# Early modulation in quarter chunks with three of four summed on VectorE, and the SSD projection in four batches, in a two-block hybrid mixer and expert kernel

## The reference, cut to what matters

```python
mod = silu(c) @ ada_w + ada_b            # ada_w is 1024 x 6144: six parts of 1024
shift, scale = mod[0:1024], mod[1024:2048]   # the other four parts are used later
h = rms_norm(x, norm1_g) * (1 + scale) + shift
z = h @ w_in                             # w_in is 1024 wide in, cut in columns by use
xbc = silu(causal_conv4(z[:, 5136:6672]) + bias)   # the 1536 SSD columns, taps over tokens
```

## Time and profile before

| | us |
|---|---|
| median of 3 runs | 2037.1 |
| lowest and highest run | 2036.84, 2040.95 |
| span of the profiled execution | 2034.4 |
| TensorE busy | 1940.5 (95%) |
| VectorE busy | 499.9 (25%) |
| ScalarE busy | 339.1 (17%) |
| GpSimd busy | 83.5 (4%) |
| HBM read | 708.44 MB, 349 GB/s over the span |

### The profile page before, as it was taken

How to read it: one execution, slowest core, us unless ns; L and a number is a source line. 1 busy time by engine, 2 the same in 40 slices (tenths; PEclk the granted TensorE clock), 3 DMA queues, 4 the chain that set the end, 5 groups by cost and what they waited for, 6 DMA issues and landing times. The chain is left out here.

```text
span 2034.4 us, 24691 instructions
## 1 busy us (share of the span) xinstructions
PE 1940.5 (95%) x10254; PEld 893.1 (44%) x10254; DVE 499.9 (25%) x1033; ACT 339.1 (17%) x617; POOL 83.5 (4%) x189
## 2 busy tenths in 40 slices
PE   8999999999999999999999999999999999888888
PEld 5688656533333333333333333345455433232232
DVE  1467534421211222212121212242342200000001
ACT  2234612100000000000000000124341111101111
POOL 2010230000000000000000000100020000000000
PEclk9999999999999999999999999999999999999999
DMA  8463455999999999999999999945255999999997
GB/s 315 166 196 126 179 208 208 370 418 419 429 427 428 428 429 428 429 428 429 428 428 429 428 428 428 410 164 169 66 206 203 401 427 427 428 428 428 428 428 322
DMA packets 105443, 710.46 MB, mean 349 GB/s; under 512 B 14551, under 2 KB 26209, under 8 KB 68001
## 3 DMA queue, kind: packets, MB, share of 16 engines
q1 hardware_dynamic: 105376, 709.53, 84.9%
HBM read 708.44 MB, written 1.07 MB: 349 GB/s over the span
## 5 line engine op out<-in xcount | busy, mean ns | idle before, releaser
L2001 PE MATMUL ps<-ring,arena 128*64 128x512 f32 x1536 | 337.4, 593 | 10.3 <-DMA ring<-in_moe_w_gu 10.3
L2001 PEld LDWEIGHTS ps<-ring,arena 128*64 128x64 f32 x1536 | 108.9, 137 | 232.7 <-issue 208.3
L3309 PE MATMUL ps<-ring,arena 128*32 128x512 f32 x768 | 170.1, 609 | 20.1 <-DMA ring<-in_w_gate 18.5
L2031 PE MATMUL ps<-ring,arena 128*64 128x512 f32 x768 | 168.9, 592 | 0.0
L2063 ACT ACTIVATE arena<-arena 128x512 f32<-128x512 f32 x32 | 20.2, 630 | 755.3 <-DVE arena L2099 755.3
L2485 PE MATMUL ps<-ring 128*128 128x512 f32 (+1 forms) x320 | 137.9, 580 | 0.7 <-ACT ring L2878 0.6
L2001 PE MATMUL ps<-arena 128*64 128x512 f32 x512 | 113.2, 593 | 3.4 <-DMA arena<-in_moe_w_gu 3.4
L1267 PEld LDWEIGHTS ps<-arena 128*128 128x128 f32 x832 | 96.0, 192 | 34.5 <-issue 32.7
L3309 PEld LDWEIGHTS ps<-ring,arena 128*32 128x32 f32 x768 | 45.0, 112 | 137.6 <-issue 136.5
L1267 PE MATMUL ps<-arena 128*128 128x128 f32 x832 | 104.0, 280 | 0.2
L2031 PEld LDWEIGHTS ps<-ring,arena 128*64 128x64 f32 x768 | 54.9, 137 | 109.9 <-issue 99.7
(11 more groups left out here) (610 smaller groups left out, 1969.5 us busy)
## 6 DMA issues: line engine op xcount, KB each, us to landing
ring<-in_moe_w_gu SPq DMA_DIRECT2D x96, 2048.0 KB, 26.1
ring<-in_moe_w_down SPq DMA_DIRECT2D x48, 2048.0 KB, 29.0
arena<-in_moe_w_gu SPq DMA_DIRECT2D x31, 2048.0 KB, 24.8
ring<-in_w_gate SPq DMA_DIRECT2D x26, 2048.0 KB, 25.9
ring<-in_w_down SPq DMA_DIRECT2D x24, 2048.0 KB, 25.1
ring<-in_w_up SPq DMA_DIRECT2D x22, 2048.0 KB, 30.4
ring<-in_w_in SPq DMA_DIRECT2D x19, 2048.0 KB, 8.1
arena<-in_moe_w_down SPq DMA_DIRECT2D x15, 2048.0 KB, 31.7
```

The source lines that it names most:

```text
L2001: last = M.matmul(ps[halves[j], 4 + which, :], xgT[buf][:, k, CAP * ee:CAP * ee + CAP], w[k2][:, at:at + 512], start=(first and k == 0), s ...
L2031: last = M.matmul(ps[halves[j], 6, :], yT[:, k % KH, halves[k // KH]], w[k % KH][:, 512 * j:512 * j + 512], start=False, stop=(k == 2 * KH ...
L3309: last = M.matmul(ps[quads[e], 4 + which, :], xgT[:, k, quads[e]], w[e][k], start=(k == 0), stop=(k == KD - 1))
```

## The change

1. The four early `ada_w` chunks are no longer two of shift and two of scale, but four quarters: chunk `i` has shift columns 256i to 256i+255 in the first half of its slot and the same columns of scale in the second half. Each is loaded by two DMAs of 1 MB with rows of 1 KB (before: one DMA of 2 MB with rows of 2 KB).
2. The load order becomes ada, xbc, ada, xbc, and so on. `load` is called for five chunks before the small parameter rows (before: four).
3. Only chunk 0 is summed on TensorE. Chunks 1 to 3 are summed on VectorE (`sums`): eight instructions of 128x512 each, the first a product with a column of `cond`, the others product and sum. `spread(i)` then reduces the 128 partitions on TensorE with the same eight instructions as before.
4. The SSD projection is done in four batches of one pair `j` of slices for all twelve units (before: two pairs with the modulation in between, then the last two pairs unit by unit). `spread(j + 1)` stands within batch `j`, behind unit 10, 8 and 8. The parameter transposes stand behind unit 3 of batch 1. Only the last batch counts units for the convolution.
5. TensorE does two products of `keep_multiplying` between the transposes of `x` and the roots, and the roots before the modulation sums (before: behind them).
6. ScalarE makes the roots before `cond` (before: behind it), and copies only the first sums.
7. The slots of xbc 0, 1 and 2 are freed after batch 0, 1 and 2 (before: the first two behind pair 1, the third behind the last unit). Later counts of `s_ada` and `s_part` fall by three.

```diff
@@ Ring @@
+                elif isinstance(src, tuple):
+                    for i in range(2):
+                        sp.dma_start(ring[:, s, 2048 * i:2048 * i + 2048].rearrange("p (k n) -> p k n", k=k), src[i]).then_inc(self.full[s], 16)
...
     def add_early(i):
-        ra.add(cols(ada_w, 512 * (0, 2, 1, 3)[i]), (KD, 512), (s_ada, i + 1), (0, 3, 4, 5)[i])
+        src = tuple(cols(ada_w, D * m + 256 * i, 256) for m in range(2))
+        early.append(ra.add(src, (KD, 512), (s_dsum, i) if i else (s_ada, 1), (0, 3, 4, 5)[i], by_pe=(i == 0)))
...
-               (s_rows_done, 1) if j < 2 else (s_unit, 12), (1, 2, 0, 3)[j])
-
-    add_early(0)
-    add_early(1)
-    add_xbc(0)
-    add_xbc(1)
-    add_early(2)
-    add_early(3)
-    add_xbc(2)
-    add_xbc(3)
+               (s_rows_done, j + 1) if j < 3 else (s_unit, 12), (1, 2, 0, 3)[j])
+
+    for i in range(4):
+        add_early(i)
+        add_xbc(i)
@@ opening.sync @@
-        ra.load(sp, 4)
+        ra.load(sp, 5)
@@ opening.tensor @@
         def spread(i):
-            pe.wait_ge(s_part, i + 1)
-            for q in range(4):
+            if i:
+                pe.wait_ge(s_dsum, i)
+                pe.wait_ge(s_hk, 2 * i)
+            else:
+                pe.wait_ge(s_part, 1)
+            for b in range(4):
...
         tokens(1).then_inc(s_first, 1)
-        pe.wait_ge(s_cw, 1)
-        modulation_sums(pe, cond, 4)
+        keep_multiplying(2, 5)
         pe.wait_ge(s_dg, 1)
         for t in range(T):
             last = M.matmul(ps[:, 6, t * P:(t + 1) * P], ones[:, :], root_diag[:, t, :])
         last.then_inc(s_rsp, 1)
+        pe.wait_ge(s_cw, 1)
+        modulation_sums(pe, cond, 4)
         spread(0)
-        modulation_sums(pe, cond, 5)
-        spread(1)
-        w = [ra.take(pe), None]
-        for u in range(4):
-            unit_rows(u, w[0], 0)
-        w[1] = ra.take(pe)
-        for u in range(4):
-            unit_rows(u, w[1], 1)
-        pe.wait_ge(s_rtk, 1)
-        pe.wait_ge(s_rows, 48)
-        M.transpose(ps[:, 6, 0:96], rowsA[0:96, :], ident[0:96, 0:96])
-        M.transpose(ps[:, 6, 96:156], rowsB[0:60, :], ident[0:60, 0:60]).then_inc(s_first, 1)
-        for u in range(4, 12):
-            for j in range(2):
-                last = unit_rows(u, w[j], j)
-            if u == 5:
-                pe.wait_ge(s_cw, 2)
-                modulation_sums(pe, cond, 6)
-            if u == 6:
-                pe.wait_ge(s_hk, 4)
-                spread(2)
-            if u == 8:
-                modulation_sums(pe, cond, 6)
-            if u == 9:
-                spread(3)
-        last.then_inc(s_rows_done, 1)
-        w = [ra.take(pe), ra.take(pe)]
+        for j in range(3):
+            w = ra.take(pe)
+            for u in range(12):
+                last = unit_rows(u, w, j)
+                if j == 1 and u == 3:
+                    pe.wait_ge(s_rtk, 1)
+                    pe.wait_ge(s_rows, 48)
+                    M.transpose(ps[:, 6, 0:96], rowsA[0:96, :], ident[0:96, 0:96])
+                    M.transpose(ps[:, 6, 96:156], rowsB[0:60, :], ident[0:60, 0:60]).then_inc(s_first, 1)
+                if u == (10, 8, 8)[j]:
+                    spread(j + 1)
+            last.then_inc(s_rows_done, 1)
+        w = ra.take(pe)
         for u in range(12):
             if u >= 6:
                 pe.wait_ge(s_conv, u - 5)
-            for j in range(2):
-                last = unit_rows(u, w[j], 2 + j)
-            last.then_inc(s_unit, 1)
+            unit_rows(u, w, 3).then_inc(s_unit, 1)
@@ opening.vector @@
+        def sums(i):
+            part, w = early_parts[i % 2].rearrange("p (m n) -> p m n", m=2), ra.arrived(dve, early[i])
+            if i >= 2:
+                dve.wait_ge(s_comb, i - 1)
+            vv(V.tensor_scalar(part, w[:, 0], cond[:, 0, 0:1], None, ALU.mult))
+            for k in range(1, KD):
+                ins = V.scalar_tensor_tensor(part, w[:, k], cond[:, k, 0:1], part, ALU.mult, ALU.add)
+                if k < KD - 1:
+                    vv(ins)
+                else:
+                    ins.then_inc(s_dsum, 1)
+
+        for i in range(4):
+            if i:
+                sums(i)
+            dve.wait_ge(s_comb, i + 1)
+            mc, at = shift_scale[:, i, :, :], slice(2 * i, 2 * i + 2)
...
+            for q in range(2):
+                k = 2 * i + q
                 V.tensor_scalar(hT[:, k, :], hT[:, k, :], mc[:, 1, q:q + 1], mc[:, 0, q:q + 1], ALU.mult, ALU.add).then_inc(s_hk, 1)
```

More of the change, by code:

```diff
@@ L163, in __init__, with add @@
             self.full = [sem(f"{name}_slot{s}_full") for s in range(SLOTS)]
-            self.chunks, self.newest, self.sent, self.used = [], {}, 0, 0
-        def add(self, src, shape, released, s):
+            self.chunks, self.newest, self.sent, self.used, self.order = [], {}, 0, 0, []
+        def add(self, src, shape, released, s, by_pe=True):
             before = self.newest.get(s)
-            arrivals = 32 if isinstance(src, list) else 16
+            arrivals = 32 if isinstance(src, (list, tuple)) else 16
             if before is not None:
@@ L173, in add @@
             self.newest[s] = len(self.chunks)
+            if by_pe:
+                self.order.append(len(self.chunks))
             self.chunks.append((src, shape, released, s, arrivals, before))
+            return self.newest[s]
         def last_uses(self):
@@ L190, in load, with arrived @@
                 self.sent += 1
+        def arrived(self, eng, n):
+            src, (k, w), _, s, arrivals, _ = self.chunks[n]
+            eng.wait_ge(self.full[s], arrivals)
+            if isinstance(src, tuple):
+                return ring[:, s, :].rearrange("p (m k n) -> p k m n", m=2, k=k)
+            return slot(s, k, w)
         def take(self, pe):
-            _, (k, w), _, s, arrivals, _ = self.chunks[self.used]
-            pe.wait_ge(self.full[s], arrivals)
             self.used += 1
-            return slot(s, k, w)
+            return self.arrived(pe, self.order[self.used - 1])
     w_in, ada_w = a["w_in"][0], a["ada_w"][0]
@@ L204, in program @@
     s_rows_done = sem("ssd_weight_rows_multiplied")
+    s_dsum = sem("later_modulation_sums_ready")
+    early = []
     def add_early(i):
-        ra.add(cols(ada_w, 512 * (0, 2, 1, 3)[i]), (KD, 512), (s_ada, i + 1), (0, 3, 4, 5)[i])
+        src = tuple(cols(ada_w, D * m + 256 * i, 256) for m in range(2))
+        early.append(ra.add(src, (KD, 512), (s_dsum, i) if i else (s_ada, 1), (0, 3, 4, 5)[i], by_pe=(i == 0)))
     def add_xbc(j):
         ra.add(w_in[2 * P * j:2 * P * j + 2 * P, C_XBC:C_XBC + 12 * P].rearrange("(k p) n -> p k n", p=P), (2, 12 * P),
-               (s_rows_done, 1) if j < 2 else (s_unit, 12), (1, 2, 0, 3)[j])
-    add_early(0)
-    add_early(1)
-    add_xbc(0)
-    add_xbc(1)
-    add_early(2)
-    add_early(3)
-    add_xbc(2)
-    add_xbc(3)
+               (s_rows_done, j + 1) if j < 3 else (s_unit, 12), (1, 2, 0, 3)[j])
+    for i in range(4):
+        add_early(i)
+        add_xbc(i)
     for j in range(2):
@@ L229, in add_late @@
     def add_late(j, s):
-        ra.add(cols(ada_w, 512 * j), (KD, 512), (s_ada, j + 1), s)
+        ra.add(cols(ada_w, 512 * j), (KD, 512), (s_ada, j - 2), s)
     def add_out(k, n, released, s):
@@ L260, in program @@
     acol = ar(19712, 32)
-    shift_scale = ar(19744, 2, 2, 4)
+    shift_scale = ar(19744, 4, 2, 2)
     hn = ar(2048, T, D)
@@ L415, in spread @@
         def spread(i):
-            pe.wait_ge(s_part, i + 1)
-            for q in range(4):
-                last = M.matmul(ps[:, 7, 4 * i + q:4 * i + q + 1],
-                                early_parts[i % 2][:, q * P:(q + 1) * P], ones[:, 0:1])
+            if i:
[4 more added lines that the diff above has]
+            for b in range(4):
+                last = M.matmul(ps[:, 7, 4 * i + b:4 * i + b + 1],
+                                early_parts[i % 2][:, b * P:(b + 1) * P], ones[:, 0:1])
             last.then_inc(s_comb, 1)
@@ L507, in _ @@
     def _(act):
[L508 to L512, removed]
         act.wait_ge(s_x, 16)
@@ L516, in _ @@
             A.activation(hn[:, t, :], x_res[:, t, :], ACT.Square, accum_out=ss[:, t:t + 1]).then_inc(s_ss, 1)
+        act.wait_ge(s_const, 1)
+        act.wait_ge(s_ss, 2)
+        A.activation(rstd, ss, ACT.Sqrt, bias=eps_t, scale=1.0 / D).then_inc(s_ss, 1)
         act.wait_ge(s_first, 1)
@@ L520, in _ @@
         A.activation(cond[:, :, 0], acol[:, 0:8], ACT.Silu).then_inc(s_cw, 1)
[L521 to L524, removed]
         act.wait_ge(s_rsp, 1)
         A.activation(roots, ps[:, 6, 0:T * P], ACT.Copy).then_inc(s_rtk, 1)
-        take_sums(1)
+        act.wait_ge(s_ada, 1)
+        A.activation(early_parts[0], ps[:, 4, :], ACT.Copy).then_inc(s_part, 1)
         act.wait_ge(s_first, 3)
         A.activation(convw[:, 0:156], ps[:, 6, 0:156], ACT.Copy).then_inc(s_cw, 1)
-        take_sums(2)
-        take_sums(3)
         for u in range(12):
@@ L559, in _ @@
```

(21 more changed lines are left out.)

## The result

| us | before | after |
|---|---|---|
| median (20 runs each) | 2036.42 | 2040.41 |
| span of the profiled execution | 2034.4 | 2037.8 |
| ratio after to before, with its 95% interval | | 1.0016 (1.0010 to 1.0022) |
| TensorE busy | 1940.5 | 1937.5 |
| VectorE busy | 499.9 | 517.8 |

The changed kernel is slower by 2.0 to 4.5 us; the medians differ by 4.0 us, the profiled spans by 3.4. TensorE has 3 us less to do, and the program ends later. A single execution far off, as one of the changed kernel's 20 at 4826.93 us and one of 3490.84 us of the kernel before among the experiments, is a slow one, and the ratios leave it out.

What follows compares the result with a forecast made beforehand. VectorE's convolution, 2.0 us a unit against TensorE's 1.7, was taken to set the narrow projection's start, shifting the program's end one to one. Waiting 2.6 plus clock 1.6 gave 4.2 us slower, 2041.3 us; range 2037.5 to 2044.5.

Steps and rivals of the forecast that it cites:

- The two engines almost level: Last pass before the narrow projection: TensorE needs 1.7 us a unit, VectorE's convolution 2.0 us, so removed work helps only TensorE.
- The sums on VectorE hidden: Batches before the last: VectorE's sums, 5.7 us each, finish before their spreads are due, with 1 to 2 us to spare.
- Taking three sums off TensorE is worth less than the added batch: Path to the convolution: two of the sums stood there, some 1.9 us each, against 10.3 us for the batch.
- The clock behind the pause: After TensorE's pause of over 5 us before the narrow projection, low clock costs 1.6 us; ends 0 and 3.2 us.
- The helper's products, and the clock in the head: Before the roots: two idle products take 2.6 us, between 1.7 and 3.4, and bring the initially low clock up sooner.
- The clock did not hold: Rival: clock holds in the opening's thin stretch, the pause or both; 0.9 to 2.6 us slower, 2038.0 to 2039.7 us; chance 0.22.
- no quarter chunk was late: Rival: batches each wait 1 us for slices because chunks land late, adding up to 3 us; 2042.5 to 2044.5 us; chance 0.15.
- The shift was not lost further on: Rival: the opening's delay vanishes later because the experts' transfers already wait for something else; 2037.1 us; chance 0.10.
- The convolution did not get quicker: Rival: VectorE's convolution speeds up, 1.04 us a unit, when TensorE leaves PSUM alone; 2030.9 us; chance 0.06.
- The bound: Whole program: a measurement can tell about 0.2%, or 4.1 us, from no change; 4.2 us slower was forecast.
- The side that I gave 0.52: Whole program: the outcome that the changed kernel is slower by more than 4.1 us; chance 0.52.
- the one that I gave 0.42: Whole program: the outcome that the difference stays within 4.1 us; chance 0.42.

Runs made afterwards that it cites:

- run 2: Changed kernel with the first two gate units ahead of the wait for the ninth convolution and the narrow projection; 2032.82 us, 0.9982.
- run 3: Changed kernel with the first gate unit between units 5 and 6 of the last batch, the second behind unit 11; 2029.77 us, 0.9967.
- run 1: Changed kernel with five idle products (4.3 us) in the pause before the narrow projection; 2038.03 us, 1.0009.
- run 4: Changed kernel with pair 2 of units 9 to 11 moved from the third batch into the last pass, spread(3) behind unit 7; 2038.65 us, 1.0010.
- run 6: Kernel before with the first two gate units ahead of the narrow projection; 2036.34 us, 0.9999.
- run 7: Changed kernel without the two idle products in front of the roots; 2041.74 us, 1.0027.
- run 9: Changed kernel with one idle product in each of the two pauses between the first sums and the first unit; 2040.97 us, 1.0021.
- Run 5: Changed kernel with the three later quarter sums back on TensorE, copied by ScalarE; 2046.83 us, 1.0047.
- run 10: Kernel before, unchanged, run once more for its profile; 2035.51 us (one time).
- run 11: Changed kernel, unchanged, run once more for its profile; 2040.39 us, 1.0015.
- run 8: Kernel before with only root before cond, two idle products and roots before the sums; chunks and load order as before; 2038.13 us, 1.0005.

## Why the prediction was right

The forecast was 2041.3 us, 4.2 us above 2037.1; measured were 2040.41 us, 4.0 us above 2036.42. (The 2037.1 was the median of three runs, and the median of twenty lies 0.7 us lower.) Most steps of the sum held within half a microsecond:

| step | forecast | profile after |
|---|---|---|
| two idle products | 2.6 | 2.65 |
| first unit | 18.3 | 18.01 |
| quarter chunks 1 to 3 landed | 22.6, 33.2, 43.8 | 22.56, 32.93, 42.99 |
| one sum on VectorE | 5.7 | 6.0 |
| convolution begins | 55.65 | 55.41 |
| narrow projection begins | 73.8 | 73.68 |
| late there, waiting | 2.6 | 2.47 |
| late by the clock | 1.6 | 1.37 |
| together | 4.2 | 3.84; 3.4 at the end |

- *The two engines almost level.* This reading carried the result. Runs 2 and 3 take the wait away and win 7.6 and 10.6 us in the medians, run 1 puts work into it free of charge, run 4 moves it with the start of the last pass, and run 6 finds nothing to win where there was no wait.
- *The sums on VectorE hidden.* Held, with less slack than I wrote: the first sum ended at 28.55 us and its spread began at 29.27 us, 0.7 us later, and for the second it was 38.92 and 39.53 us, 0.6 us. I had 1.1 and 0.9 us there. Runs 7 and 9 show the limit: what TensorE gained by an earlier start was lost at these spreads.
- *Taking three sums off TensorE is worth less than the added batch.* Run 5 gives the sums 5.8 us; 1.9 us each had been forecast.
- *The clock behind the pause.* The mechanism held; the size varies. 1.6 us was read from one row. The six profiles with the pause gave 1.4, 2.2, 2.7, 2.7, 3.0 and 3.0 us, so the value I took was met by the first profile only, and most lie nearer to the upper end of 3.2 us that I had kept.
- *The helper's products, and the clock in the head.* The 2.6 us for two products was a value taken between two ends, and that 2.65 came out is partly luck: in the ten profiles that have them they took from 1.88 to 3.10 us. That the clock is low at first I had read from the lengths alone (3.64 us against 1.92 for the same sums). The recorded clock does not show it: it says 1.00 for the stretch from 11.4 to 15.0 us in the kernel before. The two don't agree, and why stays open.
- *The rivals.* The clock did not hold in any profile with the pause unfilled. No spread of the changed kernel waited for its sum, so no quarter chunk was late. The shift was not lost further on. The convolution did not get quicker.
- *The bound.* 0.21% had been forecast, just over the bound of 0.2% or 4.1 us; the ratio came out at 0.16%, just under it, with an interval to either side of it. The side that I gave 0.52 missed by a few tenths of a microsecond, and the one that I gave 0.42 came.

That 4.2 and 4.0 us agree so closely is partly luck. A second pair of profiles (runs 10 and 11) is 5.0 us apart at the delta-net projection (100.93 and 105.90 us) and 5.4 us at the end (spans of 2033.8 and 2039.2 us), because more clock was lost behind the pause. On the other side stands a term that could not be seen from the one profile of before: its opening seems to lose clock in some executions (run 6, with the same instructions there, and run 8, with the new head) and not in others (run 10 and the first). Differences between medians therefore cannot be put down to single terms as those between two profiles can.

## What to carry to other kernels

Before work is taken out of a pass, look how far the engine that follows it is behind: here VectorE was at 2.0 us a unit and TensorE at 1.7, and a last pass of 0.86 us a unit only turned TensorE's work into waiting, while the work taken out delayed VectorE's start. Wait for a buffer as late as the list allows, and put independent work ahead of it: moving two gate units ahead of one wait was worth 7.6 us, and only with it, or with run 3's order, the rest of the change brings something (3.5 us against the kernel before). The pause of 4 to 5 us on TensorE cost its length and then 1.4 to 3.0 us at half clock behind it.

## What the runs showed that I had not expected

- The same 4.97 us pause cost 1.4 us of clock in one execution and 3.0 us in another (14.51 and 16.11 us for the same two gate units), with the kernel unchanged.
- In run 6 the clock stayed at 0.50 from 14 to 30 us though TensorE was busy for 15.96 of the 18 us from 12 to 30. With the same instructions, two profiles of the kernel before have a recorded clock of half for only 3.4 us of that stretch, and first sums of 3.6 us.
- In run 2 the stretch of 0.87 us pauses between units left the clock at 1.00; in run 1 it fell among the same units (0.62 at 65 us, 0.50 from 66 us).
- While the quarter chunks load, with rows of 1 KB, the DMA engines moved 345 to 355 GB/s; with rows of 2 KB in the kernel before it was 381 to 393, both with the engines busy throughout. For 2 MB that is about 0.6 us more, where 0.8 us had been put into the forecast (estimated from these rates); over four chunks the difference is the 0.8 us by which the last quarter landed earlier than forecast (42.99 against 43.8 us).
